# A three-layer block on one core: order of the last retention, late slots, and the first weight tile

## What is computed

```python
def reference(...):
    x = first_block(x, ...)      # attention + conv branch, then silu FFN with causal conv
    return second_block(x, ...)  # two hybrid_layer, then rms_norm

def hybrid_layer(x, norm_gain, w_in, w_out, rel_bias, cos, sin):
    proj = rms_norm_2(x, norm_gain) @ w_in      # aq, ak, av, ag, rq, rk, rv, rg: 512 each
    ya = chunked_rel_attention(aq, ak, av, rel_bias)    # 8 heads of 64
    yr = chunkwise_retention(rq, rk, rv, cos, sin)      # 4 heads of 128, each normed
    y = concatenate([ya * silu(ag), yr * silu(rg)], axis=-1)
    return x + y @ w_out
```

## Time and profile before

| what | us |
|---|---|
| median of 3 runs | 1196.54 (1194.98 to 1196.62) |
| the profiled execution | 1196.49 |
| its span, first to last instruction | 1194.7 |
| PE busy | 1178.2 (99%), 5541 matmuls |
| DVE, ACT, POOL busy | 893.9 (75%), 577.9 (48%), 257.2 (22%) |
| after the last matmul | 5.9 |

### The profile page before, as it was taken

How to read it: one execution, slowest core, us unless ns; L and a number is a source line. 1 busy time by engine, 2 the same in 40 slices (tenths; PEclk the granted TensorE clock), 3 DMA queues, 4 the chain that set the end, 5 groups by cost and what they waited for, 6 DMA issues and landing times.

```text
span 1194.7 us, 14982 instructions
## 1 busy us (share of the span) xinstructions
PE 1178.2 (99%) x5541; PEld 987.9 (83%) x5541; DVE 893.9 (75%) x1461; ACT 577.9 (48%) x971; POOL 257.2 (22%) x249
## 2 busy tenths in 40 slices
PE   8999999999999999999999999999999999999998
PEld 7888788888888888888888888899878888898876
DVE  4789955665776487547776788897887878998856
ACT  6667632323443244325444477764335578654422
POOL 0220399941100000000003611111413211012300
PEclk9999999999999999999999999999999999999999
DMA  6455533333331533243333357652223376653621
GB/s 188 124 159 164 164 105 88 106 88 106 124 93 53 154 88 106 71 123 89 105 90 88 106 170 213 191 168 72 71 71 110 120 209 179 180 167 112 158 71 71
DMA packets 216717, 146.81 MB, mean 123 GB/s; under 512 B 6250, under 2 KB 205380, under 8 KB 216516
## 3 DMA queue, kind: packets, MB, share of 16 engines
q1 hardware_dynamic: 216484, 145.79, 42.1%
q10 hardware_dynamic: 160, 0.07, 0.0%
HBM read 127.49 MB, written 18.35 MB: 122 GB/s over the span
## 4 chain that ended last, share of the span: by engine, by line
PE 87%; DVE 7%; ACT 3%; issue 1%; POOL 1%; DMA 0%; ACTq 0%; DVEq 0%
PE ps L191 86%; DVE tmp L164 1%; ACT a_p L161 1%; DVE wlo L164 1%; DVE a_p L178 1%; PE ps L194 1%; DVE a_pd L182 1%; POOL b_px L164 1%; ACT whi L161 1%; DMA ca<-in_const_a_dram 0%; DVE a_zc L167 0%; DVE b_pt L164 0%; POOL b_px L172 0%; DVE h L167 0%; ACT b_pt L161 0%
## 5 line engine op out<-in xcount | busy, mean ns | idle before, releaser
L161 ACT ACTIVATE whi<-raw 128x1024 fp32r<-128x1024 f32 (+1 forms) x198 | 206.7, 1050 | 285.7 <-PE ps L191 274.6
L164 DVE TENSOR_TENSOR wlo<-raw,whi 128x1024 fp32r<-128x1024 f32 (+1 forms) x192 | 251.7, 1316 | 41.4 <-ACT whi L161 40.5
L191 PE MATMUL ps<-x0h,whi 128*128 128x512 f32 x1008 | 255.2, 391 | 1.7 <-ACT whi L161 1.7
L191 PE MATMUL ps<-x0h,wlo 128*128 128x512 f32 x1008 | 255.0, 391 | 0.0
L191 PE MATMUL ps<-x0l,whi 128*128 128x512 f32 x1008 | 254.4, 391 | 0.0
L191 PEld LDWEIGHTS ps<-x0h,whi 128*128 128x128 f32 x1008 | 187.7, 188 | 40.3 <-ACT whi L161 2.1
L191 PEld LDWEIGHTS ps<-x0l,whi 128*128 128x128 f32 x1008 | 188.6, 188 | 39.0 <-DVE x0l L167 0.2
L191 PEld LDWEIGHTS ps<-x0h,wlo 128*128 128x128 f32 x1008 | 188.0, 188 | 38.3
L164 POOL TENSOR_TENSOR sums<-sums,sq 128x512 f32<-128x512 f32 x28 | 43.3, 1558 | 427.6 <-ACT sq L161 427.6
L191 PE MATMUL ps<-x1l,whi 128*128 128x512 f32 x304 | 82.6, 390 | 1.2 <-DVE x1l L164 1.2
L191 PE MATMUL ps<-x1h,wlo 128*128 128x512 f32 x304 | 82.3, 389 | 0.0
(11 more groups left out here) (201 smaller groups left out, 1651.1 us busy)
## 6 DMA issues: line engine op xcount, KB each, us to landing
raw<-in_w_in_dram SPq DMA_DIRECT2D x98, 512.0 KB, 4.2
raw<-in_w_up_dram SPq DMA_DIRECT2D x44, 512.0 KB, 3.8
raw<-in_w_out_dram SPq DMA_DIRECT2D x24, 512.0 KB, 3.6
turned<-b_pd SPq DMA_DIRECT2D x16, 640.0 KB, 3.5
raw<-in_w_down_dram SPq DMA_DIRECT2D x16, 512.0 KB, 3.7
b_px<-turned SPq DMA_DIRECT2D x32, 160.0 KB, 3.5
b_p<-turned SPq DMA_DIRECT2D x32, 160.0 KB, 3.5
turned_a<-a_pd SPq DMA_DIRECT2D x6, 512.0 KB, 2.6
```

What stands on the lines that cost most here:

```text
L161: return AC.put(lambda e: e.activation(o, i, func, **kw), after, AC, 1)
L164: return on.put(lambda e: e.tensor_tensor(o, a, b, op), after, on, 1)
L191: return PE.put(lambda e: e.matmul(o, l, r, start=start, stop=stop), after, PE if mark else None, 1)
```

## The change

- The identity moves from ACT's queue to the head of SP's; eight warm-ups instead of nine.
- The first weight tile is split by a new function in two pieces, columns 0 to 255 (the first two k's) and the rest; each matmul waits for its piece alone.
- The low halves of conv tiles on POOL: first and third of the triples j = 0, 1, 2, instead of all of j = 0 and j = 2.
- In the retention layers tiles 23 and 19 (k and q of retention 3) come ahead of tile 28 (the first of the gates); retention 3 is at step 88 instead of 91 and writes its results into PD; the inverse root of retention 2 is on DVE, without the wait behind it; for retentions 0 and 1 the wait is four steps. Head 4 is at step 37.
- `keep_rb2` uses the bias buffer MB instead of PD; `h_final` is at steps 98 to 105.
- The out product of the first layer leaves two late slots instead of one.

```diff
+            def split_in_two(self, cut):
+                i, self.n_split = self.n_split, self.n_split + 1
+                b, w = 1024 * (i % NRAW), 1024 * (i % NW)
+                spans = [(0, cut), (cut, 1024)]
+                th = [act(WHI[:, w + a:w + e], RAW[:, b + a:b + e], after=self.raw[i]) for a, e in spans]
+                tl = [tt(WLO[:, w + a:w + e], RAW[:, b + a:b + e], f32(WHI[:, w + a:w + e]), ALU.subtract,
+                         after=[self.raw[i], t]) for (a, e), t in zip(spans, th)]
+                self.lo_read[i] = tl[1]
+                self.load()
+                return th, tl
...
-            for m in (14 + j, 10 + j, 6 + j):
-                plan_fm(win, m, on_pool=m % 2 == 0)
+            for n, m in enumerate((14 + j, 10 + j, 6 + j)):
+                plan_fm(win, m, on_pool=j < 3 and n != 1)
...
-            order += [20, 16, "v", 21, 17, "v", 22, 18, 28, 23, 19, 29, 30, 31]
+            order += [20, 16, "v", 21, 17, "v", 22, 18, 23, 19, 28, 29, 30, 31]
...
+        t_id = dma(CA[:, 0:128], const_a[:, 0:128], d_id)
         t_mix = dma(rows[0][0:8, :], mix_norm[0].rearrange("(a b) -> a b", b=128), d_mix, on=AC)
-        t_id = dma(CA[:, 0:128], const_a[:, 0:128], d_id, on=AC)
...
-        for _ in range(9):
+        for _ in range(8):
...
-                at_once(W.split())
+                w_hi, w_lo = W.split_in_two(256)
                 w0 = W.take()
+                W.hi[0] = w_hi[0]
                 product(w0, 0, X0.ks(0, 2), True, False, parts=(0, 1))
             elif c == 1:
+                W.lo[0] = w_lo[0]
                 product(w0, 0, X0.ks(0, 2), False, False, parts=(2,))
+                W.hi[0], W.lo[0] = w_hi[1], w_lo[1]
...
-                t = act(PD[:, 0:512], RB2[:, :], after=[rb["rb2"], pd_free[0]])
+                t = act(MB[:, :], RB2[:, :], after=[rb["rb2"], ms.free[0]])
...
-                kp, pb, pfree = rps.take()
+                kp, pb, pfree = rps.take() if i < 3 else (None, PD[:, 0:1280], [pd_free[0], turn_free])
...
-                rr, t4, t_read = rsqrt_of(PS[bank][:, 0:16], 16, 1.0 / 128, 1e-6, tp, on=DV if i == 3 else PO, c=c, read=DV)
+                rr, t4, t_read = rsqrt_of(PS[bank][:, 0:16], 16, 1.0 / 128, 1e-6, tp, on=DV if i > 1 else PO, c=c, read=DV)
                 bank_free[bank] = [t_read]
-                if i < 3:
-                    yield 3
+                if i < 2:
+                    yield 4
...
-                at_step(49 if i == 6 else 12 + 6 * i, head(i))
+                at_step(12 + 6 * i + (i in (4, 6)), head(i))
...
-                evs += [[2], [3], [ev_g(4)], [ev_g(5), ev_g(6), ev_g(7)]][s - 4]
-            for i, n in enumerate((66, 74, 82, 91)):
+                evs += [[2], [3], [], [ev_g(4), ev_g(5), ev_g(6), ev_g(7)]][s - 4]
+            for i, n in enumerate((66, 74, 82, 88)):
...
-                    at_step(90 + 2 * k, h_final(k))
+                    at_step(98 + k, h_final(k))
...
-        out_tiles(8, 1, lambda m: NG2(m), [None], 4)
+        out_tiles(8, 2, lambda m: NG2(m), [None], 4)
```

More of the change, by code:

```diff
@@ L1103, in block_then_hybrid_layers @@
         p_bufs, p_free = [PB[:, 0:1280], PB[:, 1280:2560], PX[:, :]], [[], [], []]
-        hps, pxs, rps = Slots(p_bufs, [0], p_free), Slots(p_bufs, [2, 1], p_free), Slots(p_bufs, [0, 1, 2, 0], p_free)
+        hps, pxs, rps = Slots(p_bufs, [0], p_free), Slots(p_bufs, [2, 1], p_free), Slots(p_bufs, [0, 1, 2], p_free)
         ptbs = Slots([PTB[:, :]])
@@ L1409, in h_final @@
             def h_final(k):
-                h_tok[k] = stt(Hk(k), Hk(k), FIN(k), PD[:, 0:512], ALU.mult, ALU.mult, after=[rb2c, h_read[k]])
-                pd_free[0] = [h_tok[k]]
+                h_tok[k] = stt(Hk(k), Hk(k), FIN(k), MB[:, :], ALU.mult, ALU.mult, after=[rb2c, h_read[k]])
+                ms.free[0] = [h_tok[k]]
                 yield
@@ L1501, in ret @@
                 t3 = tt(t, out, s2, ALU.mult, after=[t6, ts2, free])
-                rps.free[kp] = [t3]
+                if i < 3:
+                    rps.free[kp] = [t3]
+                else:
+                    pd_free[0] = [t3]
                 s2s.free[k3] = [t3]
```

## The result

The changed kernel takes 1186.12 us (median of 4 runs, 1185.44 to 1189.54), the kernel before 1195.94 beside it: a ratio of 0.9924, 95% interval 0.9903 to 0.9945. That is 9.8 us less, clear of the noise though under 1%, where 8.1 were forecast. The profiled execution is one of 1185.57 us with a span of 1183.8, against 1194.7 before: 10.9 us less. PE is busy for 1172.0 us instead of 1178.2.

The account below looks back on a forecast made before the run. PE was taken as the bound nearly everywhere, gains only where it waits or runs at half clock: start 2.05, convolution 0, heads 0.8, first layer 1.25, second layer 4.0, sum 8.1; 1196.49 to 1188.4 us, range 1185.8 to 1192.4.

Parts of the forecast that it names:

- the conv case: Rival, convolution stage: its waits for probabilities go too, 2.2 us more saved, 1186.2 us; chance 0.12.
- Start, 2.05: Kernel start: transposes 1.4 us earlier by the identity, 0.65 us by the smaller first weight piece; bounds 0 to 3.7.
- the plain shift: Kernel start: the 2.05 us taken unchanged, between half kept (1.0) and an extra half-rate stretch spared (3.7 in all).
- Convolution, 0: Convolution stage: spreading low halves between POOL and DVE leaves the 2.2 us of waits; bounds 2.2 gained or 2.2 lost.
- DVE's idle time, which I named as cover: Convolution, third triple: the tile moved to DVE costs 1.2 us, hidden where DVE waits 2.04 us for ACT before 82.62.
- Heads, 0.8: Both retention layers: head 4 one step later removes a 0.4 us wait for q's low half in each, 0.8 us.
- First layer, 1.25: End of first retention layer: two late slots remove PE's 1.25 us wait for X1 slot 6.
- Second layer, 4.0: Second layer's end: bank wait 2.26 falls to 0.1, scores give 0.2, half clock gone gives 1.7; bounds 0.2 to 4.2.
- DVE's idle 3.9 us: Second layer's end: DVE's waits of 1.92 us for the last q's halves and 1.59 for POOL's root would go.
- What would show it: Signs in the changed profile: transposes from 5.0, first product near 8.0, named waits gone, full clock, a_pt waits of 2.2 unchanged.
- the bank's 0.1 us of margin: Second layer's end: PSUM bank emptied 0.1 us before PE needs it; rival with wait back, 1189.6 or 1192.4, chance 0.18.
- the one in which POOL's new pieces hold DVE steps: Rival, convolution: two new POOL pieces each hold DVE 2.2 us, clock falls three times, 1197.9 us; needs 4 us lag; chance 0.04.

Follow-up runs that it names:

- the start alone: Kernel before with identity first on SP, eight warm-ups instead of nine, first weight tile split in pieces of 256 and 768 columns: 1192.46 us, ratio 0.9974.
- the old placing: Changed kernel with the convolution's low halves on POOL as in the kernel before (plan indexes 6, 7, 8, 12, 13, 14): 1186.68 us, ratio 0.9925.
- The run with three steps: Changed kernel with retention 3's q and k behind the first gate, step 91, retention 2's root on POOL, retentions 0 and 1 waiting three steps: 1190.03 us.
- the old placing with 18 on POOL: Changed kernel with low halves on POOL as in the kernel before, plus plan index 18, a gate's tile: 1183.32 us, ratio 0.9889.

## Why the prediction was right, and where it wasn't

**The time.** 1186.1 lies in the range of 1185.8 to 1192.4, 2.3 under the forecast, and outside the 1187.3 to 1189.5 that I gave the forecast itself. It is nearest to the time of a rival that did not come: 1186.2, if the convolution's waits went too. They grew. So the time alone would have pointed to the wrong case; two terms were off in opposite directions, the start (2.9 more) and the convolution (1.15 less). That the range holds the time is luck in part: its lower end doesn't follow from its own terms, since the conv case with the start at its bound of 3.7 would be 1184.5.

**Start, 2.05: 4.95.** The shift was right: transposes from 5.04 (forecast 5.0), about 0.5 for the piece (0.65), first product at 7.66 (near 8.0). The mis-sized term is the clock: about 3.0, where I had put nothing above the shift. I chose the plain shift between 0 and 3.7, and even the bound was too low, since I took from the earlier trace rows that one stretch of 3.3 us at half rate could be spared; the stretch in the kernel before ran from 6.4 to 16.1 us. What I missed is that nine warm-ups ended 1.1 us ahead of the identity: moving the identity closed that pause. The pause had been listed as a wait and was worth more than its length. The run with 4 warm-ups (1.4 us later) and the one with 14 (1.2 earlier) show it from both sides. By medians the start alone is worth 3.1 us, not 4.95.

**Convolution, 0: 1.15 lost.** Two steps failed. The first is that the two pieces that go to POOL come ahead of a point at which DVE waits for PE anyhow: the piece at 46.67 helps to hold DVE's step of 44.58 (5.03 us), and the 0.90 us that DVE waits for PE before 63.40 in the kernel before is gone, so about 1.3 us of lag is handed on to unit 2. The other is that the piece of the third triple stays on POOL and so its collision stays the same. It stays, but with another partner: in the kernel before it held a `tmp` step, now it holds the maxima `smx`, which ACT's exponentials wait for. DVE's idle time, which I named as cover, lies behind the exponentials and can't cover what holds them. The sentence on the rivals that DVE and POOL meet where both read SBUF was right. The Trainium skill, "SBUF — State Buffer", section "Who interferes with whom", has the sharper rule: the pair of ports that DVE and POOL share is an exclusive lock, a DVE instruction with two SBUF inputs contends for it with a POOL instruction that reads SBUF, and the order of issue decides who is blocked. The trace agrees: POOL's piece ends at 68.28 (65.88 and 2.40), and two steps on 4 columns that began at 66.71 end at 68.50. So a collision is priced by what is left of the POOL piece, not by the size of the DVE step.

**Heads, 0.8: 0.84.** Right; undoing the step brings 0.42 back in each layer.

**First layer, 1.25: 1.25.** Right in sum, and incomplete: under the new order the second late slot takes away 2.96, of which 1.7 are the order's own.

**Second layer, 4.0: about 4.1.** The size was right (wait 2.26 to 0.10, where I had 0.1; no half clock) and the mechanism in good part wrong, so the size is luck. I counted DVE's idle 3.9 us away by the early q and k and by the root on DVE. In the changed kernel 1.92 of it are still there, the root's place is worth 0.02 us of wait, and order and root together 0.67. The one edit that I named in the change and never priced carries 1.5 us when it is undone last: the fourth step behind the earlier roots, which moves two DVE steps into the time in which DVE stood. Whether early q and k with three steps would have reached 0.1 as well is open. A step that moves in a queue needs its own price, and this one had none.

**What would show it.** No waits on `b_sets`, `x1l` and `tmp`, the clock at its upper level in the layers, no DVE wait for POOL after 1126: all as written. Waits on `a_pt` unchanged: wrong. No rival came whole; the bank's 0.1 us of margin held. Of the one in which POOL's new pieces hold DVE steps the mechanism came in part: steps were held, and the lag of unit 7 grew by 1.4 us (10.68 to 12.11), not by the 4 that it asks for.

## What to carry to other kernels

Price a pause of PE by its length and, apart from that, by the stretch at the lower clock behind it: here closing a pause at the start was worth more by the clock (1.2, 1.4 and about 3.0 us in three comparisons) than by its 1.1 us, and warm-up work should reach right up to the first real instruction. Before a step is given to POOL, look at what DVE does in those 2.4 us: a two-input step on SBUF that others wait for loses up to the whole piece, and the same half on DVE costs 1.2. When several edits meet in one queue, price each by what it puts into an idle time, not only by what it takes away, and undo them one after another, since here the smallest edit carried 1.5 of 2.16 us when it was undone last; undo them in more than one order before the shares are called settled.

## What the hardware showed that I had not expected

The clock behind a wait. PE's wait of 1.02 us between 121 and 127 us stands in the kernel before, in the changed kernel and in eleven of the twelve experiments. In five of these thirteen profiles the granted clock falls to 0.50 right behind it (the old placing, 123.40 to 126.70 above: eight matmuls from 123.19 take 3.45 us), in eight it doesn't. The changed kernel's window at that place, at full clock:

```profile
123.10:126.40 3.30, 3.30 (x15) 2.71 (x16) 2.94 (x6) 2.76 (x6) 0.00 (x0) 1.00 0.59 183
```

Behind the waits of 2.26 and 2.96 us it fell in all five profiles that have one. The run with three steps shows what a fall is worth: its profiled execution has two falls more than the wait at 1139 explains (at 9.3 and 125.4 us) and took 1193.48 us, its other three executions 1189.89 to 1190.07: 1.7 us for each, if those three had only the one fall (they have no profile). What decides whether a wait of about 1 us brings a fall isn't settled by these runs. Nor does a wait of that length by itself spread the times: the old placing with 18 on POOL has one of 1.02 us and took 1183.06 to 1183.54, the changed kernel 1185.44 to 1189.54.
